# Hi products of both banks first, then lo products of both, in the 512-column products of a two-block transformer kernel

## What is computed

```python
x = x + 0.5 * swiglu(rms_norm(x, ffn1_norm), ffn1_wg, ffn1_wu, ffn1_wd)   # phase ffn1, d_ff 2816
x = x + hybrid_mixer(rms_norm(x, mix_norm), ...)                          # phases mixin and gates
x = x + 0.5 * swiglu(rms_norm(x, ffn2_norm), ffn2_wg, ffn2_wu, ffn2_wd)   # phase ffn2
x = rms_norm(x, final_norm)
x = x + gmlp_mixer(rms_norm_2(x, a_norm_g), ...)                          # phases vgate and gmlp
k, v = shared_kv(x, g_kv, w_kv)
x = x + chunk_attention_mixer(rms_norm_2(x, b_norm_g), k, v, ...)         # phase chunk
return rms_norm_2(x, final_norm_g)

def swiglu(x, wg, wu, wd):
    return (jax.nn.silu(x @ wg) * (x @ wu)) @ wd
```

## Time and profile before

| | |
|---|---|
| Time, median of 3 runs (lowest to highest) | 858.19 us (857.57 to 858.28) |
| The profiled execution's own time | 858.39 us |
| its span, first to last instruction | 856.6 us |
| PE busy / PEld busy | 848.3 us (99%) / 738.0 us (86%) |
| DVE busy / ACT busy / POOL busy | 637.6 (74%) / 524.8 (61%) / 59.6 us (7%) |
| Granted clock of PE, mean | 0.998 |
| Read from HBM | 160.65 MB, 189 GB/s over the span |

### The profile page before, as it was taken

The page is one execution under the profiler, slowest core; times in us unless marked ns, Lnnn a source line. Parts: engine busy times, 40 slices in busy tenths (PEclk is TensorE's granted clock), DMA queues, the critical chain, the costliest instruction groups (busy, mean ns, idle before and its releaser), DMA issues.

```text
span 856.6 us, 11976 instructions
## 1 busy us (share of the span) xinstructions
PE 848.3 (99%) x4775; PEld 738.0 (86%) x4775; DVE 637.6 (74%) x788; ACT 524.8 (61%) x738; POOL 59.6 (7%) x65
## 2 busy tenths in 40 slices
PE   9999999999999999999999999999999999999997
PEld 8988888888889898888888887888888898888885
DVE  5999999987698656765466468758777677877873
ACT  6677777766575544653554356548666665576772
POOL 0022222210000000000000000100000001000001
PEclk9999999999999999999999999999999999999999
DMA  8976566554544655576456545586655655853501
GB/s 271 351 238 201 179 197 197 194 159 158 204 148 141 204 193 177 172 252 231 155 165 231 195 148 187 195 284 224 203 197 193 210 179 168 262 177 108 191 1 50
DMA packets 123991, 162.47 MB, mean 190 GB/s; under 512 B 3864, under 2 KB 111136, under 8 KB 123808
## 3 DMA queue, kind: packets, MB, share of 16 engines
q1 hardware_dynamic: 122320, 154.89, 55.0%
q0 software_dynamic: 1312, 6.29, 2.2%
q10 hardware_dynamic: 304, 0.53, 0.2%
HBM read 160.65 MB, written 1.05 MB: 189 GB/s over the span
## 4 chain that ended last, share of the span: by engine, by line
PE 98%; DVE 1%; ACT 0%; POOL 0%; issue 0%; POOLq 0%; DVEq 0%
PE pAcc L448 23%; PE pG L392 9%; PE pU L392 9%; PE pAcc L392 7%; PE pG L395 5%; PE pR L392 5%; PE pU L395 5%; PE pM L392 4%; PE pAcc L395 3%; PE pR L395 2%; PE pAcc L428 2%; PE pAcc L427 2%; PE pAcc L426 2%; PE pM L395 2%; PE pG L509 1%; PE pM L428 1%
## 5 line engine op out<-in xcount | busy, mean ns | idle before, releaser
L326 DVE TENSOR_TENSOR lo<-raw,hi 128x2048 fp32r<-128x2048 f32 x131 | 298.5, 2288 | 52.7 <-ACT hi L321 52.7
L321 ACT ACTIVATE hi<-raw 128x2048 fp32r<-128x2048 f32 x140 | 265.5, 1907 | 18.4 <-PE pAcc L428 5.6
L392 PE MATMUL pG<-xT,hi 128*128 128x512 f32 x336 | 83.7, 391 | 0.0
L392 PE MATMUL pU<-xT,hi 128*128 128x512 f32 x320 | 80.2, 392 | 0.0
L448 PE MATMUL pAcc<-hi,h_hi 128*128 128x512 f32 x240 | 74.8, 393 | 0.0
L448 PE MATMUL pAcc<-lo,h_hi 128*128 128x512 f32 x240 | 74.2, 390 | 0.0
L448 PE MATMUL pAcc<-hi,h_lo 128*128 128x512 f32 x240 | 74.0, 389 | 0.0
L392 PEld LDWEIGHTS pG<-xT,hi 128*128 128x128 f32 x336 | 62.1, 188 | 13.0 <-issue 0.7
L1110 ACT ACTIVATE h_hi<-h 128x512 fp32r<-128x512 f32 x28 | 17.7, 633 | 81.2 <-PE pAcc L448 75.4
L392 PEld LDWEIGHTS pU<-xT,hi 128*128 128x128 f32 x320 | 57.5, 189 | 10.3
L1629 DVE TENSOR_TENSOR h_lo<-h,h_hi 128x512 fp32r<-128x512 f32 x28 | 19.3, 689 | 46.5 <-ACT h_hi L1110 46.5
(11 more groups left out here) (505 smaller groups left out, 1639.3 us busy)
## 6 DMA issues: line engine op xcount, KB each, us to landing
raw<-in_a_w_in SPq DMA_DIRECT2D x24, 1024.0 KB, 5.3
raw<-in_ffn_wd SPq DMA_DIRECT2D x22, 1024.0 KB, 5.3
raw<-in_ffn_wg SPq DMA_DIRECT2D x21, 1024.0 KB, 5.3
raw<-in_ffn_wu SPq DMA_DIRECT2D x21, 1024.0 KB, 6.2
raw<-in_w_in SPq DMA_DIRECT2D x16, 1024.0 KB, 5.5
raw<-in_a_w_out SPq DMA_DIRECT2D x8, 1024.0 KB, 5.0
raw<-in_w_kv SPq DMA_DIRECT2D x8, 1024.0 KB, 5.5
raw<-in_b_w_qz SPq DMA_DIRECT2D x8, 1024.0 KB, 5.6
```

The lines of the kernel that those rows point to most:

```text
L321: act.activation(HI[n % NHL][:, :], RAW[n % NRAW][:, :], ACT.Copy).then_inc(S["hi"], 1)
L326: dve.tensor_tensor(LO[n % NHL][:, :], RAW[n % NRAW][:, :], HI[n % NHL][:, :].bitcast(f32), ALU.subtract).then_inc(S["lo"], 1)
L392: pe.matmul(v3(bank[:, :], 2), wh[:, k, w], x4[:, :, k, :], start=(k == 0), stop=False, skip_group_check=True)
```

## The change

In `wide_to_features` the order of the four groups of eight matmuls changes from hi(bank 0), lo(bank 0), hi(bank 1), lo(bank 1) to hi(bank 0), hi(bank 1), lo(bank 0), lo(bank 1). The number and kind of the matmuls stay the same. The wait for `free[1]` moves ahead of the lo products of bank 0; `wide` is still raised by the last lo matmul of bank 0 and `used` by that of bank 1. Nothing is changed on the other engines.

```diff
-            for f, bank in enumerate(banks):
-                pe.wait_ge(*free[f])
-                w = slice(f * P, (f + 1) * P)
+            def of_hi(bank, f):
                 for k in range(KD):
-                    pe.matmul(v3(bank[:, :], 2), wh[:, k, w], x4[:, :, k, :], start=(k == 0), stop=False,
+                    pe.matmul(v3(bank[:, :], 2), wh[:, k, f * P:(f + 1) * P], x4[:, :, k, :], start=(k == 0), stop=False,
                               skip_group_check=True)
+
+            def of_lo(bank, f):
                 for k in range(KD):
-                    end = pe.matmul(bank[:, 0:TOK], wl[:, k, w], x4[:, 0, k, :], start=False, stop=(k == KD - 1),
-                                    skip_group_check=True)
-                end.then_inc(S["used" if f else "wide"], 1)
+                    end = pe.matmul(bank[:, 0:TOK], wl[:, k, f * P:(f + 1) * P], x4[:, 0, k, :], start=False,
+                                    stop=(k == KD - 1), skip_group_check=True)
+                return end
+
+            pe.wait_ge(*free[0])
+            of_hi(banks[0], 0)
+            pe.wait_ge(*free[1])
+            of_hi(banks[1], 1)
+            of_lo(banks[0], 0).then_inc(S["wide"], 1)
+            of_lo(banks[1], 1).then_inc(S["used"], 1)
```

## The result

The changed kernel takes 866.4 us where the kernel before took 858.24 us beside it: ratio 1.0096 (95% interval 1.008 to 1.0113), slower by about 1%. Two of its four runs, with TensorE's clock at 0.75 and 0.58 on average, are left out, and none of four runs on another chip was like them. Those four gave 866.78 us beside 858.17 us, ratio 1.0103 (1.0086 to 1.0119). The profiled execution took 866.47 us, its span 864.7 us.

What follows compares the result with a forecast made beforehand. TensorE's matmul stream was taken to bound the kernel. 7.7 + 0.26 + 0.95 - 1.2 = +7.7 us on 858.39 us gave 866.1, adjusted to 865.9 us; own range 864.3 to 867.6, 8-in-10 range 862.0 to 870.0.

Steps and rivals of the forecast that it cites:

- The chain in an iteration: From gate block start T in ffn1, late G and U sums delay the up block: 0.96 us each, eight lose 7.7.
- The start after a wait: In ffn1, TensorE restarts 0.05 us after DVE's sum; eight hi with unloaded weights then take 1.93 us.
- a further 0.1 us at each wait: Upper bound on TensorE's restart delay: at each of 17 waits, adding 1.7 us to the forecast.
- Iterations with four bias steps: ffn1 iterations with four bias steps: VectorE's work ends 0.25 us before G's copy is ready, so no cost.
- rival 3: VectorE becomes ffn1's bound: half a microsecond more in each of eight iterations, 869.9 us; chance 0.12.
- The end of ffn1: Last gate block: 0.26 us at `to_features` into G, then 0.95 us waiting for `h_lo_last`, weights included.
- The 61 others: Calls outside ffn1: later emptying costs nothing and each keeps its 0.02 us saving, -1.2 us together.
- The clock: TensorE's clock in ffn1 stays at 1.00 despite pauses; the rival, a fall, gives 879 us, chance 0.02.

Runs made afterwards that it cites:

- ffn1_old: The changed kernel with the old order in all 17 ffn1 calls, the new order in the other 61; 857.02 us, ratio 0.9988.
- lo_after_light: lo_after with VectorE's bias sums of head 2 also cut to 16 of 512 columns; 861.03 us, ratio 1.0032.
- gate_only: The kernel before with the new order only in ffn1's nine gate blocks; 863.81 us, ratio 1.0067.
- after_pool: The changed kernel with GpSimd's bias additions for head 3 cut to 16 of 512 columns; 866.23 us, ratio 1.0094.
- last_old: The changed kernel with the old order in one call, the last gate block of ffn1; 865.58 us, ratio 1.0086.
- lo_after: The changed kernel with VectorE's `lo` moved behind the sum of U in eight ffn1 iterations; 870.49 us, ratio 1.0146.
- gate_old: The changed kernel with the old order in ffn1's nine gate blocks, the new order in 69 calls; 860.52 us, ratio 1.0027.
- gate_old_pool: gate_old with GpSimd's bias additions for head 3 cut to 16 of 512 columns; 858.76 us, ratio 1.0006.

## Why the prediction was right

It said 865.9 us; 866.4 and 866.8 us were measured, within its narrower range of 864.3 to 867.6 us. In the trace, from the first wide call on, the time grew by 8 x 0.98 + 3 x 0.22 + 1.35 - 1.12 = 8.73 us, where 7.7 us was forecast. The start-up was 0.6 us shorter than in the kernel before, which leaves the 8.1 us between the two spans. Against the forecast's steps, one by one:

- **The chain in an iteration.** Copy at T + 4.83 (4.84 measured), sum of G at 5.25 to 5.67 (5.26 to 5.68), sum of U to 8.21 (8.22), PE on U at 8.26 (8.27), end at 12.10 (12.13). 0.96 us was forecast, 0.98 measured; `ffn1_old` shows that it is all of ffn1's making, `lo_after_light` that the `lo` makes the U wait, `gate_only` that the earlier demand for U has its share.
- **The start after a wait** was the step that was off. The up block started at T + 5.83 and not 5.72: 0.15 us behind DVE's end, and the matmul behind `h_lo_last` 0.15 us too (195.02 - 194.87). Behind the sum of U it was the 0.05 us of the earlier trace rows (117.19 - 117.14). The error at G cost nothing, since U was the later one; it was in the bounds ("a further 0.1 us at each wait").
- **Iterations with four bias steps.** The prediction gave VectorE 0.25 us of margin there and no cost, with rival 3 as what would come if something ate it. Something did: `after_pool` shows 0.12 us of margin left, less than thought (h_lo hands over after 0.60 us, 131.40 to 132.00 in the changed kernel, so at 132.27 in `after_pool`, and G's sum starts at 132.39), and GpSimd's addition takes 0.34 us. Three times 0.22 us, 0.66 us, is missing from the sum. So a sixth of rival 3's 4 us is in the result. Its mechanism was named; that the bias sums grow longer when they come to lie beside GpSimd's additions was not.
- **The end of ffn1**: 0.26 + 0.95 = 1.21 us forecast, 1.31 to 1.35 us measured, with h's sum at T + 12.94 (12.92 forecast) and `h_lo_last` ending at T + 15.14 (15.13). `last_old` takes it all away. The difference is the 0.15 us of above.
- **The 61 others**: -1.2 us forecast, -1.12 measured, and no single one lost more than 0.01 us. So the rule "Evacuate promptly" of the Trainium skill ("PSUM — Partial Sum Buffer", section "Summary: rules for kernel authors") is not borne out as a rule on time here: in 61 of 78 calls a bank emptied 1.8 us later costs nothing, in 17 it costs 9.9 us.
- **The clock** stayed at 1.00 through ffn1 with PE held up by 0.3 to 0.9 us at a time, as the forecast had it. `lo_after` shows a fall behind 1.95 us of waiting. The Trainium skill's "TensorE: Matmul & The Clock Gate", section "A second HAM failure mode: psum-queue depth-cycling", would have small pauses between bank groups bring the clock down; with sixteen small delays in a row in ffn1 the trace shows none.

Right for the reason given, then, with errors of one sign that add up to 1.0 us (0.66 us at the iterations with four steps, 0.16 us in the eight iterations, some 0.14 us at the end of ffn1, 0.08 us at the others). That the first median lies only 0.5 us above the forecast is in part luck: the start-up of the profiled execution was 0.6 us shorter, which no step of the forecast accounts for. What my expectations got wrong for `gate_old`, `gate_old_pool`, `gate_only` and `lo_after` was neglect of VectorE in iterations with four steps and of when the untouched block asks for its bank.

## What to carry to other kernels

Before two groups of matmuls are put in another order, write down for each bank when it is complete, the whole chain that frees it, and when it is next asked for: here one turn saved 0.02 us a call, and the shorter cover cost 0.98 us wherever the next call wanted the same bank at once, 0.64 us of it by another block's `lo` that stood between the two sums (0.71 us with it, 0.07 without). Apply such an order only where the bank has other work behind it; in the phases with that, it kept its gain (857.02 for 858.19 us). And ask of a second engine not only whether it waits, but how many tenths of a microsecond it has to give in its fullest iteration, with the work of its neighbours moved along.

## What the hardware showed that I had not expected

- **VectorE beside GpSimd.** The bias sum with all operands in SBUF took 0.74 or 0.75 us alone, and 1.09 and 1.32 us where a 1.29 us addition of GpSimd had begun before it; the sums with an operand in PSUM (`pM`, `pR`) kept their 0.75 us beside it. The addition's row reached 0.20, 0.53 and 0.77 us into such sums, and they took 0, 0.34 and 0.57 us more: each time 0.2 us less than the rows overlap, as if VectorE stood still until shortly before the addition's end. Where VectorE's sum had begun first, it was the addition that grew, to 1.53 us (128.93 in the changed kernel), and the sum kept its 0.74 us. The Trainium skill's "SBUF — State Buffer", section "Who interferes with whom", says that a VectorE instruction with two SBUF inputs contends with a GpSimd instruction that reads SBUF, and one with at most one SBUF input doesn't. The trace agrees with both halves.
- **TensorE's clock fell mid-kernel** to 0.50 after a wait of 1.95 us for VectorE, three times out of three in `lo_after`; the waits of up to 0.9 us in the other kernels were without a fall. (A wait of 1.5 us stands in every kernel's start-up, before the clock first rose, at 7.29 us in the kernel before.)
- **Two release times.** From the end of DVE's sum to PE's next matmul 0.15 us passed at G and at `h_lo_last`, and 0.05 us at U, in the same kernel. At G and at `h_lo_last` the row of the first weight load starts 0.03 us ahead of the matmul (114.72, 194.99), at U together with it (117.19). What separates the two is open; no run was made for it.
